# Who builds the one-hots while experts are selected, and who begins the key spreads

## The reference

```python
q = (xb @ w_q).reshape(PEER_TOKEN_BLOCK, PEER_HEADS, 2, PEER_HALF)
s = jnp.einsum('thcd,hcnd->thcn', q, sub_keys).astype(jnp.float32)
s_top, i_top = lax.top_k(s, PEER_TOPK)
cand_idx = i_top[:, :, 0, :, None] * PEER_KEYS + i_top[:, :, 1, None, :]
best, pos = lax.top_k(cand, PEER_TOPK)
expert = jnp.take_along_axis(cand_idx, pos, axis=-1)
gates = jax.nn.softmax(best, axis=-1).astype(xb.dtype)
act = jax.nn.gelu(jnp.einsum('td,thkd->thk', xb, u_tab[expert]))
return jnp.einsum('thk,thkd->td', gates * act, v_tab[expert])
```

## Time and profile before

| | us |
|---|---|
| median of three runs | 2358.3 |
| lowest and highest | 2356.89 and 2359.77 |
| span of the profiled execution, first to last instruction | 2357.1 |
| busy: PE, PEld, DVE | 2254.7, 1934.6, 1777.9 |
| busy: ACT, POOL | 748.7, 745.3 |
| chain that ended last | PE 70%, DMA 15%, DVE 9%, POOL 2%, ACT 2% |

### The profile page before, as it was taken

One profiled execution on the slowest core, in us unless ns is written; L12 is line 12 of the kernel. 1 busy time (PEld: TensorE's weight loads), 2 busy tenths in 40 slices (PEclk: granted clock), 3 DMA queues, 4 the chain that ended last, 5 costly groups with the idle time before them and its releaser, 6 DMA issues.

```text
span 2357.1 us, 30495 instructions
## 1 busy us (share of the span) xinstructions
PE 2254.7 (96%) x11914; PEld 1934.6 (82%) x11914; DVE 1777.9 (75%) x3437; ACT 748.7 (32%) x1028; POOL 745.3 (32%) x688
## 2 busy tenths in 40 slices
PE   8999999999999999999999999999778899999991
PEld 7888888889999998989888888888777666766661
DVE  8666777678999897665798897656889865666669
ACT  4345556544344433444111111111566301000000
POOL 0000000000000000000566644566457555666665
PEclk9999999999999999999999999999999999999996
DMA  6544444546854443565898998999820499999998
GB/s 225 184 187 169 162 175 157 197 167 187 244 177 166 162 174 143 183 225 218 307 408 318 413 390 343 414 410 414 316 86 28 166 414 415 413 414 414 413 414 331
DMA packets 128591, 633.09 MB, mean 269 GB/s; under 512 B 14656, under 2 KB 14656, under 8 KB 86080
## 3 DMA queue, kind: packets, MB, share of 16 engines
q1 hardware_dynamic: 48816, 346.64, 38.5%
q0 software_dynamic: 74736, 275.81, 30.6%
q10 hardware_dynamic: 4896, 8.70, 1.2%
HBM read 626.84 MB, written 4.26 MB: 268 GB/s over the span
## 4 chain that ended last, share of the span: by engine, by line
PE 70%; DMA 15%; DVE 9%; POOL 2%; ACT 2%; issue 1%; ACTq 0%; DVEq 0%; POOLq 0%
PE ps L1019 19%; DMA work<-in_peer_v_rows,weight_raw 14%; PE ps L709 14%; PE ps L712 7%; PE ps L663 6%; PE ps L686 5%; PE ps L687 5%; PE ps L693 5%; PE ps L978 4%; DVE scan_ws L2236 3%; DVE work L2221 2%; POOL work L613 2%; DVE ps L2193 1%; PE ps L1056 1%; DMA scan_ws<-second_kept 1%
## 5 line engine op out<-in xcount | busy, mean ns | idle before, releaser
L2236 DVE SCALAR_TENSOR_TENSOR scan_ws<-work,weight_raw,scan_ws 128x1024 f32<-128x1024 f32 x254 | 326.4, 1285 | 156.1 <-DMA work<-in_peer_v_rows,weight_raw 151.2
L1065 PE MATMUL ps<-weight_raw,pairs 128*128 128x512 f32 x1024 | 440.9, 593 | 1.9 <-DMA weight_raw<-in_peer_v_dense 1.2
L1019 PE MATMUL ps<-work,weight_raw 128*128 128x256 f32 x2048 | 442.5, 379 | 0.0
L1019 PEld LDWEIGHTS ps<-work,weight_raw 128*128 128x128 f32 x2048 | 389.1, 190 | 52.6
L1065 PEld LDWEIGHTS ps<-weight_raw,pairs 128*128 128x128 f32 x1024 | 303.7, 297 | 137.2 <-DMA weight_raw<-in_peer_v_dense 1.9
L1680 DVE TENSOR_TENSOR weight_low<-weight_raw,weight_high 128x2048 fp32r<-128x2048 f32 x145 | 332.0, 2290 | 102.0 <-ACT weight_high L1163 101.9
L613 POOL DMA_INDIRECT work<-in_peer_v_rows,weight_raw x256 | 314.4, 1228 | 183.2 <-DVE scan_ws L2236 121.5
L709 PE MATMUL ps<-operand_parts,weight_high 128*128 128x512 f32 x1456 | 354.9, 396 | 3.4 <-DVE slots L1666 1.2
L709 PEld LDWEIGHTS ps<-operand_parts,weight_high 128*128 128x128 f32 x1456 | 268.9, 188 | 61.1 <-issue 7.5
L1163 ACT ACTIVATE weight_high<-weight_raw 128x2048 fp32r<-128x2048 f32 x145 | 276.7, 1908 | 76.8 <-PE ps L712 71.2
L2184 DVE SCALAR_TENSOR_TENSOR work<-work,scan_ws 128x1024 f32<-128x1024 f32 x184 | 222.3, 1225 | 104.5 <-DMA work<-in_peer_u_rows,weight_raw 102.4
(11 more groups left out here) (292 smaller groups left out, 2662.7 us busy)
## 6 DMA issues: line engine op xcount, KB each, us to landing
weight_raw<-in_w_in SPq DMA_DIRECT2D x120, 1024.0 KB, 4.8
weight_raw<-in_peer_u_dense SPq DMA_DIRECT2D x64, 1024.0 KB, 8.1
weight_raw<-in_peer_v_dense SPq DMA_DIRECT2D x64, 1024.0 KB, 8.0
weight_raw<-in_w_out SPq DMA_DIRECT2D x32, 1024.0 KB, 4.8
weight_raw<-in_peer_w_q SPq DMA_DIRECT2D x13, 1024.0 KB, 7.6
weight_raw<-in_conv_w_out SPq DMA_DIRECT2D x8, 1024.0 KB, 4.9
weight_raw<-in_ssm_w_val SPq DMA_DIRECT2D x8, 1024.0 KB, 4.7
weight_raw<-in_ssm_w_gate SPq DMA_DIRECT2D x8, 1024.0 KB, 4.8
```

The lines of the kernel that those rows point to most:

```text
L1019: mm = nc.tensor.matmul(ps[:, 6 + s % 2, h * T:(h + 1) * T], w[:, h, k, :], gained_u[:, k, :], start=(k == 0), stop=(k == KU - 1))
L1065: mm = nc.tensor.matmul(ps_v[:, t, c, :], pairs[:, i // QKEYS, t * P:(t + 1) * P, i % QKEYS], w[:, i % 2, c * 512:(c + 1) * 512], start=(i ...
L2236: v.scalar_tensor_tensor(out=y_tok[:, t, :], in0=row_at(s), scalar=pick_w[:, g:g + 1], in1=y_tok[:, t, :], op0=ALU.mult, op1=ALU.add).then ...
```

## The change

Six spread buffers instead of two: four more lie in the first 2048 columns of `work`. Chunks 0 to 17 (`WIDE_CHUNKS`) use the six in turn, the later ones the old two. SyncE issues all spreads: 0 and 1 before u slab 48, 2 to 7 when the last u slab is used, and ahead of the v slabs 0, 1, 2 and 3 those up to 11, 15, 19 and 31, each when the chunk that used its buffer has been read. Of the chunks 1, 3, ... 17 (`POOL_CHUNKS`) GpSimd builds the one-hots, in one operation of 1024 elements: add minus the partition, compare with zero. Chunk 1 stands before u gather 250 on its queue, 3, 5, 7 and 9 before 252, 253, 254 and 255, then 11 and 13, the one-hots of placing group 0, chunk 15, those of group 1, chunk 17. ScalarE keeps the even chunks and those from 18 on, with its two operations, and does chunk 0 before it copies the last u slab. The v rows 0 and 1 are gathered with 2 and 3, ahead of group 8. Semaphores are merged so that there are enough of them.

```diff
+CHUNKS_ALL = T // CHUNK_T
+SPREADS, WIDE_CHUNKS = 6, 18
+SPREAD_OF = [c % SPREADS if c < WIDE_CHUNKS else c % 2 for c in range(CHUNKS_ALL)]
+POOL_CHUNKS = list(range(1, WIDE_CHUNKS, 2))
+ACT_CHUNKS = [c for c in range(CHUNKS_ALL) if c not in POOL_CHUNKS]
...
-        spread = scan_ws[:, 2048:3072].bitcast(BF16).rearrange("p (a b) -> p a b", a=2)
+        spread = [scan_ws[:, 2048 + 512 * n:2560 + 512 * n].bitcast(BF16) for n in range(2)] \
+            + [work[:, 512 * n:512 * n + 512].bitcast(BF16) for n in range(SPREADS - 2)]
...
+            def spread_second(c):
+
+                b = SPREAD_OF[c]
+                if b in SPREAD_OF[:c]:
+                    spread_read(sp, max(e for e in range(c) if SPREAD_OF[e] == b))
+                elif b > 1:
+                    sp.wait_ge(u_done, PAIR_SLABS)
+                src = d["second_kept"].rearrange("t p n -> (t p n)")[c * CHUNK_T * P:(c + 1) * CHUNK_T * P]
+                sp.dma_start(spread[b], src.unsqueeze(0).broadcast_to([P, CHUNK_T * P])).then_inc(spread_in[b], 16)
...
+                elif s == 3 * CLAIM:
+                    sp.wait_ge(second_kept, 16 * TT)
+                    for c in range(2):
+                        spread_second(c)
+            for c in range(2, 8):
+                spread_second(c)
             for s in range(PAIR_SLABS):
+                if s < RING:
+                    for c in range(8 + 4 * s, 12 + 4 * s):
+                        spread_second(c)
+                elif s == RING:
+                    for c in range(8 + 4 * RING, CHUNKS_ALL):
+                        spread_second(c)
...
+            def chunk_compared(c):
+
+                spread_landed(pool, c)
+                if c == 1:
+                    pool.wait_ge(row_free[3], U_USES[3])
+                else:
+                    pool.wait_ge(chosen, 2 * (c - 1))
+                hot = turned_hot[:, c % 2, :, :].rearrange("p t n -> p (t n)")
+                nc.gpsimd.tensor_scalar(hot, spread[SPREAD_OF[c]], minus_key, 0.0, ALU.add, ALU.is_equal).then_inc(pool_hot_ready, 1)
+
             for g in range(TT * PICKS):
+                if g in (250, 252, 253, 254, 255):
+                    chunk_compared((250, 252, 253, 254, 255).index(g) * 2 + 1)
...
-            for g in range(2):
-                value_row(g)
             pool.wait_ge(keys_copied, TT)
+            for c in (11, 13):
+                chunk_compared(c)
             for n, g in enumerate(POOLED):
                 if g == 8:
-                    for early in (2, 3):
+                    for c in range(WIDE_CHUNKS - SPREADS + 2, WIDE_CHUNKS):
+                        spread_read(pool, c)
+                    for early in range(4):
                         value_row(early)
...
+                if g < 2:
+                    chunk_compared(15 + 2 * g)
...
-            def spread_second(c):
-
-                src = d["second_kept"].rearrange("t p n -> (t p n)")[c * CHUNK_T * P:(c + 1) * CHUNK_T * P]
-                act.dma_start(spread[:, c % 2, :], src.unsqueeze(0).broadcast_to([P, CHUNK_T * P])).then_inc(spread_in[c % 2], 16)
-
             def second_compared(c):
 
-                act.wait_ge(spread_in[c % 2], 16 * (c // 2 + 1))
-                if c >= 2:
+                spread_landed(act, c)
+                if c == 0:
+                    act.wait_ge(row_free[2], U_USES[2])
+                else:
                     act.wait_ge(chosen, 2 * (c - 1))
                 hot = turned_hot[:, c % 2, :, :].rearrange("p t n -> p (t n)")
-                nc.scalar.activation(hot, spread[:, c % 2, :], ACT.Abs, bias=minus_key).then_inc(spread_abs, 1)
-                act.wait_ge(spread_abs, c + 1)
-                if c + 2 < T // CHUNK_T:
-                    spread_second(c + 2)
+                nc.scalar.activation(hot, spread[SPREAD_OF[c]], ACT.Abs, bias=minus_key).then_inc(spread_abs, 1)
+                act.wait_ge(spread_abs, ACT_CHUNKS.index(c) + 1)
                 nc.scalar.activation(hot, hot, ACT.Relu, bias=one_c, scale=-1.0).then_inc(hot_ready, 1)
```

More of the change, by code:

```diff
@@ L115 @@
 TILES = TILE_WQ + 16
+SLABS = 64 + 16 + 56 + 8 + 16 + 16
 PLAIN = 2
@@ L380, in build @@
         raw_landed = [sem(f"raw_landed{b}") for b in range(NSLAB)]
-        params_in, ssm_in, b_in, c_in, subk_in = (sem(n) for n in ("params_in", "ssm_in", "b_in", "c_in", "subk_in"))
+        params_in, ssm_in, matrices_in = (sem(n) for n in ("params_in", "ssm_in", "matrices_in"))
         gain_turned, gain_spread, gain_ready = sem("gain_turned"), sem("gain_spread"), sem("gain_ready")
@@ L412, in build @@
         x_kept, x_back_in = sem("x_kept"), sem("x_back_in")
-        tail_landed = [sem(f"tail_landed{n}") for n in range(RING)]
         u_done, u_evicted, v_done = sem("u_done"), sem("u_evicted"), sem("v_done")
         second_ready, second_kept, keys_turned, keys_copied = sem("second_ready"), sem("second_kept"), sem("keys_turned"), sem("keys_copied")
-        spread_in = [sem(f"spread_in{n}") for n in range(2)]
+        spread_in = [sem(f"spread_in{n}") for n in range(SPREADS)]
         second_hot_ready, act_hot_ready, act_abs = sem("second_hot_ready"), sem("act_hot_ready"), sem("act_abs")
-        spread_abs, hot_ready = sem("spread_abs"), sem("hot_ready")
+        spread_abs, hot_ready, pool_hot_ready = sem("spread_abs"), sem("hot_ready"), sem("pool_hot_ready")
         chosen, chosen_summed = sem("chosen"), sem("chosen_summed")
@@ L432, in freed, with spread_landed, spread_read, tail_count @@
             return n + PSLOTS
+        def spread_landed(eng, c):
+            b = SPREAD_OF[c]
+            eng.wait_ge(spread_in[b], 16 * (SPREAD_OF[:c].count(b) + 1))
+        def spread_read(eng, c):
+            if c in POOL_CHUNKS:
+                eng.wait_ge(pool_hot_ready, POOL_CHUNKS.index(c) + 1)
+            else:
+                eng.wait_ge(spread_abs, ACT_CHUNKS.index(c) + 1)
+        def tail_count(n):
+            return 16 * (SLABS // NSLAB + n // RING + 1)
         M_B = 0
@@ L504, in _ @@
                     sp.dma_start(w_q_early[n], w_q[PRELOADED[n]]).then_inc(q_landed[n], 16)
+            assert len(slab_ends) == SLABS and SLABS % NSLAB == 0
             def load_tail(n, src):
-                sp.dma_start(w_raw[:, n % RING, :], src).then_inc(tail_landed[n % RING], 16)
+                sp.dma_start(w_raw[:, n % RING, :], src).then_inc(raw_landed[n % RING], 16)
             for n, t in enumerate(QUERY_RING):
@@ L1012, in pair_tiles @@
                 n = U_AT + s
-                pe.wait_ge(tail_landed[n % RING], 16 * (n // RING + 1))
+                pe.wait_ge(raw_landed[n % RING], tail_count(n))
                 if s > 1:
@@ L1025, in choose @@
                 c = g // 2
-                if g % 2 == 0:
-                    pe.wait_ge(hot_ready, c + 1)
+                if g % 2 == 0 and c in POOL_CHUNKS:
+                    pe.wait_ge(pool_hot_ready, POOL_CHUNKS.index(c) + 1)
+                elif g % 2 == 0:
+                    pe.wait_ge(hot_ready, ACT_CHUNKS.index(c) + 1)
                 if g >= 4:
@@ L1097, in _ @@
             pe.wait_ge(first_out, 2)
-            pe.wait_ge(subk_in, 16)
+            pe.wait_ge(matrices_in, 48)
             score(ps[:, 5, :], 0, 0).then_inc(first_scored, 1)
@@ L1331, in ssm_matrices @@
                 elif n == 12:
-                    act.wait_ge(c_in, 16)
+                    act.wait_ge(matrices_in, 32)
                     c_im = ct[:, 1].rearrange("p a b -> p (a b)")
@@ L1563, in _ @@
                     keys_out(1)
-                elif s == 3 * CLAIM:
-                    act.wait_ge(second_kept, 16 * TT)
-                    for c in range(2):
-                        spread_second(c)
+                elif s == PAIR_SLABS - 1:
+                    second_compared(0)
                 act.wait_ge(u_done, s + 1)
@@ L1572, in _ @@
             chunks = GROUPS_T // 2
-            for c in range(chunks + 2):
-                if c < 2:
-                    act.wait_ge(row_free[2 + c], U_USES[2 + c])
+            for c in ACT_CHUNKS[1:ACT_CHUNKS.index(chunks + 2)]:
                 second_compared(c)
@@ L1830, in _ @@
             input_tile(LAM_AFTER + 3)
-            dve.wait_ge(b_in, 16)
+            dve.wait_ge(matrices_in, 16)
             own.do(v.memset(b_diag, 0.0))
```

11 lines of the change are left out of this document (7 added, 4 removed).

## The result

The changed kernel takes 2367.55 us (median of five, 2367.2 to 2370.45), the one before, timed with it, 2358.44: ratio 1.0041 [1.0029, 1.0053], slower by 9.1 us by the medians and 9.7 by the ratio. The forecast was 2354.9, with a range from 2349.5 to 2362.5. The profiled execution spans 2367.9 against 2357.1.

The account below looks back on a forecast made before the run. The end waits for gathered rows, so time won in selecting, bound by ScalarE's passes and spread arrivals, should come out whole. Gains 3.5 + 1.7 + 1.7 less 3.1 and 0.4 give 3.4 us: 2358.3 to 2354.9, range 2349.5 to 2362.5.

Parts of the forecast that it names:

- The comparison at 2.0 us: In selecting, GpSimd's new operation of 1024 elements takes 2.0 us, between 1.55 and 4.8.
- Row 255 late by 3.1 us, and 254 in time: End of selecting: gather 255, queued behind chunk 9, costs 3.1 us (1.5 to 6); gather 254 lands in time.
- Idle time of the first eight chunks, a gain of 1.7: Selecting: spreads issued by SyncE win back VectorE's 1.7 us idle; its work of 3.30 us per chunk is the floor.
- The start, a gain of 3.5: Start of selecting: with slabs held behind spreads, VectorE's first group begins at 1673.9, not 1677.4; gain between 1.1 and 3.5.
- A gain of 1.7 behind the rows: Selecting after the last gathered row: 16 groups need 17.2 us instead of 18.9, a gain of 1.7.
- The table load in front of the gelu: On ScalarE after selecting: the 1.28 us load falls under earlier idle time, counted only in the all-short case.
- everything short: Faster rival: comparison 1.5 us, row landing 5.0, table load hidden, better placing rhythm; 2350.5 us, chance 0.2.
- Placing, a cost of 0.4: Placing: two more gathers before group 8 take GpSimd 2.6 us, a later wait absorbs 2.4; from gain 2 to cost 2.6.
- The last stretch, unchanged: From the last placed group to the end, 500 us: fixed bytes, so it changes by no more than 1 us.
- The rival of the port: Slower rival in selecting: long GpSimd comparisons block VectorE's row products through the shared port; 2366 us, chance 0.16.

Follow-up runs that it names:

- one step: Changed kernel with GpSimd's comparison in one arithmetic step (equal to the partition's number) instead of two: 1.0007 [0.9988, 1.0027] against the kernel before.
- ScalarE alone: Changed kernel with ScalarE building all one-hots, no GpSimd comparison of 1024 elements, SyncE still issuing the spreads: 0.9970 [0.9951, 0.9988] against the kernel before.
- the ninth: Changed kernel with ScalarE building all one-hots and SyncE issuing all spreads ahead of the second table's first slab: 2350.88 us, 0.9966 against the kernel before.
- all spreads first: Changed kernel with SyncE issuing all spreads ahead of the first slab of the second table: 1.0021 [1.0002, 1.0040] against the kernel before.
- both orders: Changed kernel with all spreads ahead of the slabs and u gathers 252 to 255 each one comparison earlier: 1.0010 [0.9987, 1.0032] against the kernel before.

## Why the prediction was wrong

The sign was wrong, and the time fell above the range. By its steps:

- **The comparison at 2.0 us: wrong, and the first cause.** It measured 3.71, stretched up to 4.32, and shortening it to 2.85 alone took back 9.1 of the 12.6 us lost behind the first reduction. I had bounds of 1.55 and 4.8 and took the slope of the 384-element memset, which reads nothing, and explained away the 597 ns of the small comparison by a large fixed part. The fixed part is 0.27 to 0.29 us. The row of the same kind of operation, scaled with its length, was the better guide: 597 x 8 = 4.8 is above what was measured by 1.1, 2.0 is below by 1.7. An estimate from the Trainium skill (GPSIMD Engine Reference, section 3.1: 1.8 cycles at best for one input) gives 1.5 ns per element; the runs show 2.5 for one step and 3.3 for two, so in this case the page's figure was a lower bound only.
- **Row 255 late by 3.1 us, and 254 in time: the right gather, but the loop ahead of it and the size wrong.** The waits are 4.02, 0.40 and 6.45, and the stretch from the first reduction to row 255 grew by 10.7 us. Row 255 was multiplied at 1714.05 against a forecast landing at 1702.3. Of these 11.7 us, 7.1 are that group 15 was chosen at 1700.8 and not at 1693.7: 2.6 the later start; 1.1 idle time up to group 11; and 3.4 GpSimd's own loop, since chunk 7's comparison ended only at 1697.66 and the products behind it took 3.10 us at the lower clock. I had let VectorE's banks set that moment (1692.55; they were free at 1696.3), because with 2.0 us GpSimd's loop came to 4.3 a pair. In truth its comparisons began 6.2 and then 7.6 us apart (1687.10, 1693.34, 1700.98). The wait for row 253 is not on this path: it ran beside GpSimd's loop, and ended before row 255 was wanted. On top come 2.1 us of a longer comparison (4.14 for 2.0) and 2.1 of landing (8.73 for 6.6). I had seen that a slab is issued at the same moment and answered it by leaving out the low end; it should have been priced, by the 10.2 us of landings under slabs.
- **Idle time of the first eight chunks, a gain of 1.7: the floor was right, the gain was not had.** With ScalarE alone it is (3.30 per chunk to the end, no wait). Here part of it went already in chunk 2. Its spread was taken at 3.3 us and early enough; it was issued at 1671.95, and ScalarE's Abs began at 1679.15, after 5.76 us idle. By the kernel the Abs waits only for that spread and for chunk 0's products, which had ended at 1675.48, so the spread took about 7.2 us.
- **The start, a gain of 3.5: 1.2 in this profile (6.2 to 5.0), 3.4 in most others.** The slabs were indeed away (335 GB/s from 1658 to 1672, 413 before), but rows 246 and 247 were still waited for, 1.19 and 1.33 us. They landed about 6 us after their issue and not 10, but GpSimd issued them late: at 1666.52 and 1668.81, 1.99 us each. In eight of the nine variants of the changed kernel the rows were there, TensorE decided, and the first reduction came 2.8 us after the dense end, where the forecast had 2.6 to 2.7; in the ninth it came after 6.6. So the size was right where its condition held, and whether it holds differs from execution to execution. That the slabs held back give it is not borne out. The kernel before has 5.3 with its slabs held back and 5.4 without that, and in the first of these traces the last row had been multiplied 15 us ahead of the dense end. The 2.5 us from there to 2.8 are thus not the rows'; more likely they are the first one-hots, made under the last slab. That was not tried alone.
- **A gain of 1.7 behind the rows: a loss.** From the end of row 255 to the turning of the sums it took 21.3 us against about 19.1 in the kernel before. Two causes are in the chain: TensorE at 1.2 GHz after 6.88 us without work (6.60 for 4.1, so 2.5 us), and GpSimd in one line, chunk 13, one-hots of group 0, chunk 15: 3.7 + 2.3 + 3.7. Their exact shares were not measured apart; the clock at least is a consequence of the row wait.
- **The table load in front of the gelu** was hidden, as the case "everything short" wanted; nothing else of that case held.
- **Placing, a cost of 0.4:** it got 1.8 us shorter, within the bounds given. Moving the rows alone made it 1.7 longer in the kernel before. Neither is more than the 119.7 to 123.0 that traces of the same placing show, so a cost or gain of this size is not shown either way.
- **The last stretch, unchanged:** 499.9 against 498.9. A microsecond won or lost ahead of it did come out at the end whole.
- **The rival of the port** came near the number (2366) with the wrong mechanism. In the changed kernel all row products stayed at 1.22 to 1.23 us, and some of GpSimd's comparisons were longer (3.93, 3.96, 4.32, 4.14 in place of 3.71); that VectorE stretched them is likely, but not shown. The mark that I had set for it, row products of 2 to 4 us, stayed away in this kernel. In the kernels with one step, with all spreads first and with both orders it did appear, for one or two products and about 1 us each, so the port costs something, but far less than the rival had it. The Trainium skill (SBUF — State Buffer, section "Who interferes with whom") has the pair of ports locked for the whole instruction. The runs agree in part: a product beside a comparison was held for about 0.9 to 1.3 us and then ran to its end while the comparison was still going, and other products ran beside one without any loss.

The marks of the two profiles add up: 0.3 of the dense half, -1.2 at the start, +10.7 to row 255, +1.9 from there to placing, -1.8 in placing and +0.9 behind (-0.1 and +1.0), 10.8 together: the difference of the spans. By experiments, about 17 us is the price of GpSimd's share (order, slab beside it, clock and pace), and about 7 the gain of all the rest of the change together; how much of the 7 is SyncE's spreads and how much the first one-hots under the last slab was not tried apart.

## What to carry to other kernels

Price an operation that the trace does not show from the nearest row of the same kind scaled with its length, not from a cheaper kind; change its length once to find the fixed part before believing in one. When work is put on an engine that also issues DMAs in strict order, follow each DMA through the new work, as well as what is issued by the same event elsewhere. Ask which loop releases that work: here comparison and products follow one another, and the gather leaves when the loop has gone round often enough, whatever the engine that waits for it does. An engine's share in the chain doesn't justify moving its work: here ScalarE alone was faster once its spreads no longer hung on its own queue. And compare one trace with another only from a mark behind which their states agree.

## What was not expected of the hardware

- GpSimd's comparison from bf16 to f32 costs 3.34 ns per element with two steps and 0.29 us fixed; with one step 2852 ns for 1024 elements, about 2.52 ns per element if the short one from f32 lies on the same line.
- A gather of 512 KB landed in 5.6 to 6.0 us with no slab beside it, and in 8.7 to 9.1 beside a slab of 1 MB issued within 0.3 us of it.
- The issue of such a gather takes GpSimd between 0.94 and 1.99 us, and then 0.30 until the next. A pause before it does not decide: four in a row took 1.99, 1.99, 1.00 and 0.94 (from 1666.52, changed kernel), and one after 4.22 us of idle time took 1.82 (1675.32, kernel before). What decides was not tried.
- TensorE's granted clock stayed at 1.00 in the first part of a wait of 6.88 us (1709.70 to 1712.00), was 0.50 from 1713.00 on, and was still 0.50 for its next products, which lost 2.5 us where the wait itself was over. It was 0.50 elsewhere too: from 1700.80 to 1706.00, with waits of 2.76 and 2.02 us around one chunk's products, and from 1675.00 to 1678.40 in the kernel before, after 3.67 us without work.
- VectorE and GpSimd side by side: in some places a row product took up to 2.49 us instead of 1.22, in some a comparison took 3.93 to 4.32 instead of 3.71, and in some neither was longer. No product was held for the whole length of the comparison beside it.
